# The mixer layers' token-major groups claim their PSUM banks one by one, with ScalarE's copies and VectorE's maxima and sums in TensorE's bank order

## What is computed

```python
m_t = jnp.maximum(inter, dmat.max(axis=-1))
sw = jnp.exp(dmat - m_t[..., None]) * jnp.einsum('bhntk,bhnsk->bhnts', qc, kc)
num = einsum(sw, vc) + s_inter[..., None] * einsum(qc, c_prev)
h = num / jnp.maximum(jnp.abs(den), jnp.exp(-m_t))[..., None]
```

## Time and profile before

| | |
|---|---|
| median of 3 runs | 3080.92 us (3078.48 to 3084.71) |
| span of the profiled execution | 3079.1 us |
| TensorE busy | 97% of the span, 14046 matmuls |
| VectorE, ScalarE, GpSimd busy | 48%, 21%, 65% |
| DMA | mean 89 GB/s |

### The profile page before, as it was taken

One profiled execution on the slowest core, in us unless ns is written; L12 is line 12 of the kernel. 1 busy time (PEld: TensorE's weight loads), 2 busy tenths in 40 slices (PEclk: granted clock), 3 DMA queues, 4 the chain that ended last, 5 costly groups with the idle time before them and its releaser, 6 DMA issues.

```text
span 3079.1 us, 37943 instructions
## 1 busy us (share of the span) xinstructions
PE 2987.8 (97%) x14046; PEld 2451.0 (80%) x14046; DVE 1466.0 (48%) x2397; ACT 649.8 (21%) x1436; POOL 1999.0 (65%) x2041
## 2 busy tenths in 40 slices
PE   8989999999999998999999999999999999999998
PEld 6867778788888877778788888778878888888886
DVE  6668784533324777876443322566321221224543
ACT  3256333200001336433210000000111121211000
POOL 6755454877777766444777777787766555555775
PEclk9999999999999999999999999999999999999999
DMA  4322221433333322222333333233333223222332
GB/s 148 97 69 65 66 68 56 133 92 95 96 94 127 96 83 79 63 63 61 114 96 95 95 95 103 89 96 101 92 95 99 74 82 96 76 83 69 96 96 75
DMA packets 87066, 274.65 MB, mean 89 GB/s; under 512 B 10384, under 2 KB 11024, under 8 KB 86928
## 3 DMA queue, kind: packets, MB, share of 16 engines
q1 hardware_dynamic: 85392, 270.71, 28.7%
q10 hardware_dynamic: 1536, 2.10, 0.3%
HBM read 266.48 MB, written 4.19 MB: 88 GB/s over the span
## 4 chain that ended last, share of the span: by engine, by line
PE 89%; DVE 7%; ACT 2%; issue 1%; POOL 0%; DMA 0%; DVEq 0%; SPq 0%; ACTq 0%; POOLq 0%
PE PS L495 59%; PE PS L544 13%; PE PS L774 5%; PE PS L782 3%; PE PS L845 2%; PE PS L822 1%; PE PS L833 1%; PE PS L1069 1%; PE PS L508 1%; ACT TB L1179 1%; PE PS L1044 0%; DVE SMALLS L1694 0%; PE PS L1036 0%; DVE SQ L1726 0%; PE PS L582 0%
## 5 line engine op out<-in xcount | busy, mean ns | idle before, releaser
L465 POOL TENSOR_TENSOR WL<-RAW,WH 128x512 fp32r<-128x512 f32 (+2 forms) x538 | 796.9, 1481 | 9.8
L457 POOL TENSOR_TENSOR POOL_C<-POOL_C 128x1 f32<-128x1 f32 x538 | 128.5, 239 | 1011.5 <-PE PS L495 580.2
L495 PE MATMUL PS<-XNH,WH 128*128 128x512 f32 x1752 | 693.5, 396 | 3.1 <-DVE OQK L2257 1.6
L495 PE MATMUL PS<-XNL,WH 128*128 128x512 f32 x1752 | 684.3, 391 | 0.0
L462 POOL TENSOR_TENSOR WL<-RAW,WH 128x512 fp32r<-128x512 f32 x420 | 582.8, 1388 | 35.0
L458 POOL TENSOR_SCALAR WH<-RAW 128x1024 fp32r<-128x1024 f32 (+3 forms) x538 | 529.6, 984 | 0.6 <-issue 0.3
L495 PE MATMUL PS<-XNH,WL 128*128 128x512 f32 x1752 | 434.3, 390 | 0.1
L495 PEld LDWEIGHTS PS<-XNH,WH 128*128 128x128 f32 x1752 | 328.9, 188 | 76.1 <-issue 8.2
L495 PEld LDWEIGHTS PS<-XNL,WH 128*128 128x128 f32 x1752 | 329.2, 188 | 71.1 <-issue 3.1
L495 PEld LDWEIGHTS PS<-XNH,WL 128*128 128x128 f32 x1752 | 327.5, 187 | 69.6 <-POOL WL L465 1.0
L544 PE MATMUL PS<-WH,XNH 128*128 128x512 f32 x704 | 279.8, 398 | 7.0 <-ACT VEXT L1179 2.9
(11 more groups left out here) (375 smaller groups left out, 4548.1 us busy)
## 6 DMA issues: line engine op xcount, KB each, us to landing
RAW<-w_oslot SPq DMA_DIRECT2D x56, 512.0 KB, 3.6
RAW<-w_L0ffn SPq DMA_DIRECT2D x44, 512.0 KB, 3.6
RAW<-w_L1ffn SPq DMA_DIRECT2D x44, 512.0 KB, 3.6
RAW<-w_od SPq DMA_DIRECT2D x32, 512.0 KB, 3.6
RAW<-w_L0G SPq DMA_DIRECT2D x24, 512.0 KB, 3.6
RAW<-w_L1G SPq DMA_DIRECT2D x24, 512.0 KB, 3.6
RAW<-w_epg SPq DMA_DIRECT2D x16, 512.0 KB, 3.6
RAW<-w_eug SPq DMA_DIRECT2D x16, 512.0 KB, 3.6
```

Source lines behind the costliest of these rows:

```text
L457: nc.gpsimd.tensor_tensor(POOL_C[:, 1:2], POOL_C[:, 0:1], POOL_C[:, 0:1], ALU.add)
L465: nc.gpsimd.tensor_tensor(WL[:, half, at_:w], RAW[:, slot, at_:w], WH[:, half, at_:w].bitcast(F32), ALU.subtract).then_inc(S("weights_spli ...
L495: mm = nc.tensor.matmul(bank, w[:, slot, k * cols:(k + 1) * cols], x[:, k0 + k, :], start=first and j == 0 and w is WH and x is hi, stop=l ...
```

## The change

`token_group` no longer claims its four banks ahead; each tile claims its own before its first high pass. `spread_u(0)` is issued within the `mo` group, before its last chunk. The second `kvup` group uses the banks in the order 1, 4, 2, 3 and `dv` in the order 5, 0, 1, 4, and ScalarE's copies follow. In the loop `n1` goes to bank `b`, out of which the turned weights were just copied, in place of bank 1. ScalarE copies the turned weights of tile 0 ahead of the key scalings, and the first two `dk` tiles ahead of the exponentials of tile 2. VectorE does `maxima(0)` before the last tile of `dq`, `total` before `maxima` and `state`, and reads `n2` before it rotates a tile of `sk`.

```diff
@@ by_tokens, token_group (TensorE)
-            def by_tokens(outs, c, slot, ks, cols, hi, lo, n_k, shared=False, tiles=range(NT)):
+            def by_tokens(outs, c, slot, ks, cols, hi, lo, n_k, shared=False, tiles=range(NT), banks=None):
                 for w, n in turns:
+                    if banks is not None and w is WH:
+                        claim(banks[n])
             def token_group(name, banks, cols=T, k_per=2, n_k=KD, hi=XNH, lo=XNL, at=0, halfway=None):
-                claim(*banks)
                 for q in range(n_k // k_per):
                     by_tokens([PS[b][:, 0:cols] for b in banks], c, c % 2,
-                              range(q * k_per, (q + 1) * k_per), cols, hi, lo, n_k)
+                              range(q * k_per, (q + 1) * k_per), cols, hi, lo, n_k,
+                              banks=banks if q == 0 else None)
@@ layer (TensorE)
-                token_group(f"L{li}mo", (1, 2, 3, 4))
...
-                spread_u(0)
+                token_group(f"L{li}mo", (1, 2, 3, 4), halfway=lambda: spread_u(0))
...
-                token_group(f"L{li}kvup", (1, 2, 3, 4), k_per=2, n_k=2, hi=CKVH, lo=CKVL, at=1)
+                token_group(f"L{li}kvup", (1, 4, 2, 3), k_per=2, n_k=2, hi=CKVH, lo=CKVL, at=1)
...
-                    claim(1, 0)
+                    claim(b, 0)
                     pe.wait_ge(*L("swt_copied", n + 1))
                     for h in range(M_HEADS):
-                        mm = nc.tensor.matmul(PS[(1, 0)[h // 2]][:, h % 2 * 129:h % 2 * 129 + 129],
+                        mm = nc.tensor.matmul(PS[(b, 0)[h // 2]][:, h % 2 * 129:h % 2 * 129 + 129],
-                    release[1] = release[0] = L("tot_ready", n + 1)
+                    release[b] = release[0] = L("tot_ready", n + 1)
...
-                token_group(f"L{li}dv", (0, 1, 4, 5))
+                token_group(f"L{li}dv", (5, 0, 1, 4))
@@ layer (ScalarE); the copies out of kvup and dv follow the new bank orders too
                 for n in range(NT):
-                    if n:
-                        step_exponentials(n)
                     if n == 2:
                         chunk(seg("dkA") + 4)
                         for m in range(2):
                             run(DKR[:, m, :], PS[4 + m][:, :], ACT.Copy, L("dk_raw"), scale=RTOK[:, m:m + 1])
+                    if n:
+                        step_exponentials(n)
...
                     if n == 0:
                         root("sk", squares=False)
-                        act.wait_ge(*L("rk_ready", 1))
-                        scale_keys(0)
                     act.wait_ge(*L("swt_ready", n + 1))
                     if n:
                         act.wait_ge(*L("n1_ready", n))
                     run(SWT, PS[6 + n % 2][:, :], ACT.Copy, L("swt_copied"))
+                    if n == 0:
+                        act.wait_ge(*L("rk_ready", 1))
+                        scale_keys(0)
@@ layer (VectorE)
-                squares(S_HEADS, "dq")
-                dq_tables = rope_tables(row("dq_g"), 1)
-                for n in range(NT):
-                    norm_tile(DQR, n, RSH, dq_tables, "dq")
...
-                    for e, b in enumerate((1, 0)):
+                    for e, b in enumerate((6 + n % 2, 0)):
...
-                maxima(0)
+                squares(S_HEADS, "dq")
+                dq_tables = rope_tables(row("dq_g"), 1)
+                for n in range(NT):
+                    if n == NT - 1:
+                        maxima(0)
+                    norm_tile(DQR, n, RSH, dq_tables, "dq")
...
                 for n in range(NT):
                     if n:
+                        total(n - 1)
                         maxima(n)
-                        total(n - 1)
                         state(n - 1)
...
-                    if n < NT - 1:
-                        dve.wait_ge(*L("k_scaled", 8 * n + 8))
-                        norm_tile(TA, n, None, sk_tables, "sk")
                     if n:
...
                         dve.wait_ge(*L("n2_taken", n))
+                    if n < NT - 1:
+                        dve.wait_ge(*L("k_scaled", 8 * n + 8))
+                        norm_tile(TA, n, None, sk_tables, "sk")
```

More of the change, by code:

```diff
@@ L640, in layer @@
                             lambda f: L("ckv_low", f + 1))
-                token_group(f"L{li}mo", (1, 2, 3, 4))
-                for n, b in enumerate((1, 2, 3, 4)):
-                    release[b] = L("mo_ready", n + 1)
                 def spread_u(n):
@@ L650, in spread_u @@
                     release[6 + n % 2] = L("ub_taken", n + 1)
-                spread_u(0)
+                token_group(f"L{li}mo", (1, 2, 3, 4), halfway=lambda: spread_u(0))
+                for n, b in enumerate((1, 2, 3, 4)):
+                    release[b] = L("mo_ready", n + 1)
                 pe.wait_ge(*L("iq_turned", 1))
@@ L665, in layer @@
                     release[b] = L("sk_raw", n + 1)
-                token_group(f"L{li}kvup", (1, 2, 3, 4), k_per=2, n_k=2, hi=CKVH, lo=CKVL, at=1)
-                for n, b in enumerate((1, 2, 3, 4)):
+                token_group(f"L{li}kvup", (1, 4, 2, 3), k_per=2, n_k=2, hi=CKVH, lo=CKVL, at=1)
+                for n, b in enumerate((1, 4, 2, 3)):
                     release[b] = L("sv_ready", n + 1)
@@ L745, in layer @@
                             lambda f: L("tr_copied", f + 10))
-                token_group(f"L{li}dv", (0, 1, 4, 5))
-                for n, b in enumerate((0, 1, 4, 5)):
+                token_group(f"L{li}dv", (5, 0, 1, 4))
+                for n, b in enumerate((5, 0, 1, 4)):
                     release[b] = L("dv_ready", n + 1)
```

## The result

The changed kernel takes 3062.0 us (median of 4, 3060.7 to 3064.6) beside 3079.8 us of the kernel before (4 runs on the same chip, 3078.5 to 3084.7): ratio 0.9942, interval 0.9928 to 0.9956. It is 17.8 us faster. The forecast was 33.8 us, and 3062.0 lies 2 us beyond the end of its range.

The account below looks back on a forecast made before the run. It took TensorE, busy 2987.8 of 3079.1 us, as the bound. Gains of 16.0 (`mo` and `kvup`), 15.2 (loop) and 2.6 (first gate) made 33.8 us off, 3045.3, stated as a 3047 us median, range 3039 to 3060.

Parts of the forecast that it names:

- Start of mo and kvup: Groups ahead of the mLSTM loop: TensorE's waits go and `kvup` runs at full clock, 16.0 us gained.
- The loop: mLSTM loop over four token tiles: new order ends it at 46.6 us, gaining 9.1 and 6.1, together 15.2 us.
- By it the maxima, reading PSUM, keep their length in the new place: `maxima(0)` moved before the last `dq` tile: by the skill's two-SBUF-input rule, PSUM-reading maxima are not held off by GpSimd.
- Putting `total` ahead of `maxima` costs the maxima nothing: VectorE's loop order: the spread that the maxima read is issued after the product that `total` waits for; no cost.
- The walk's sum: Tile-by-tile timing of the mLSTM loop in the new order, from the end of `kvup`: 46.6 us.
- rival 1: VectorE bounds the loop and GpSimd's splits stretch it: loop 49.5 us in both layers, 3054 us; chance 0.16.
- Against: Objection to rival 1: in the loop before, most rotations' instructions were at their short length; no size given.
- The first gate: First gate after the loop: bank 5, now copied first of `dv`, removes most of its wait; gain 2.6 us.
- The clock: Without an idle stretch ahead, the `kvup` pair should run at full clock: 2.37 and 1.76 us gained.
- under 0.97: Sign that the forecast is wrong: a granted TensorE clock below 0.97 in the loop.
- rival 2: TensorE's clock falls again because new short waits in the loop come close together: 3060 us; chance 0.09.
- rival 3: Slower: a lasting clock fall in the loop; at 60% slow the time is 3101 us; chance 0.03.

Follow-up runs that it names:

- e6_total_late: The changed kernel with VectorE doing `maxima` ahead of `total` again: 3083.9 us, ratio 1.0014.
- e7_norm_early: The changed kernel with the key (`sk`) rotation ahead of the reading of `n2` again on VectorE: 3062.1 us, ratio 0.9938.
- e4_nolow: The changed kernel with only 8 columns of the `dk` weights' low parts computed on GpSimd, so its result is incomplete: 3051.1 us, ratio 0.9905.
- e5_before_nolow: The kernel before with only 8 columns of the `dk` weights' low parts computed on GpSimd: 3079.7 us, ratio 0.9995.
- e1_front: The kernel before with only the changes ahead of the loop (claims, `spread_u(0)`, `kvup` bank order, early `maxima(0)`): 3066.0 us, ratio 0.9952.
- e3_gate: The changed kernel with GpSimd's splits of three key chunks held until that tile's maxima are done: 3063.1 us, ratio 0.9940.
- e8_gate_hall: The changed kernel with three GpSimd splits held, `HALL` scaling moved to ScalarE, and `dk` sums ahead of the `HALL` products with `MO`: 3057.8 us, ratio 0.9923.
- e11_dv_order: The changed kernel with the `dv` banks in the old order 0, 1, 4, 5: 3065.6 us, ratio 0.9950.
- e2_loop: The kernel before with only the loop's changes and the new `dv` order, everything ahead of the loop as before: 3084.4 us, ratio 1.0011.

## Why the prediction was wrong, step by step

**Start of mo and kvup: right.** 14.9 us of 16.0 in the trace, and 14.8 us as a version of its own (there with loops 3.3 us shorter and a gate 2.1 us longer in it). `mo` lost its wait whole. `kvup` kept 0.41 us for ScalarE's copy out of its first bank, which the sum had at nothing. The maxima of tile 0 took 4.15 us in the new place, against 3.12, beside work of GpSimd: harmless there, but the same thing as in the loop.

**The loop: the step that failed.** The sum took the maxima at 3.03 us and masked product to masked product at 11.7 us, on the ground that "By it the maxima, reading PSUM, keep their length in the new place". Only the two instructions that read the bank do. Ten of the thirteen are 128x4 products and maxima out of SBUF, most with two SBUF inputs, and they took up to 1.28 us for 0.15. The rule on two SBUF inputs (the Trainium skill, SBUF — State Buffer, "Who interferes with whom") speaks of exactly these; the trace agrees with it, and the prediction had left these ten out. Measured: 4.6, 6.2 and 6.8 us for tiles 1 to 3 in layer 0 (3.12 by this measure in tile 3 before), and 14.9 and 15.2 us from one L707 to the next (209.15, 224.03, 239.19 for their starts). The trace of before already spoke against it: the forecast took tile 3's length for all, and tile 1 of layer 0 had taken 4.9 us. What brought the maxima onto the splits is that they start 1 us later against GpSimd, and the gap was 3.6 us wide. In tile 3 `total` makes 0.67 us of that, so the sentence "Putting `total` ahead of `maxima` costs the maxima nothing" is wrong there; but e6_total_late (stretched without it) and e7_norm_early (short with it) point to the key rotation behind the reading of `n2`. The forecast counted the rotation's own time and not what the maxima behind it would meet. e4_nolow and e5_before_nolow show the size: 11 us of the missing 16. The walk's sum was good to half a microsecond (46.1 for 46.6) once that was removed, in part by luck, since its tile 1, 1.0 us too late, made up for rounds that were 0.6 us too short.

This was rival 1, in a harder form: 54.5 and 50.8 us for its 49.5. Its "Against" (most rotations ran at their short length) looked at rotations, and where they had stood: not at the maxima, and not at where the change puts them.

**The first gate: mis-sized.** Forecast 2.6, measured 0.8. The `dv` order helps (1.9 us more waiting when undone), but the copies had been taken as tied to TensorE. They are tied to VectorE: it ends the `dk` sums, ScalarE's 7.76 us of scalings follow, and the copies come last. A shorter loop ends TensorE's work earlier; where that chain doesn't come forward as much, part of the gain turns into this wait: 1.46 to 2.5 us in e1_front, 4.5 in e3_gate, where the held splits fell onto the chain. In e4_nolow, with most of those splits gone, the chain came forward with the loop and the wait stayed at 0.8.

**The clock.** 1.00 in `kvup` and 0.97 and 0.93 in the loop, "under 0.97" being one of the wrong signs. Both loops of e3_gate and of e4_nolow stayed at 1.00, with waits of up to 2.0 and 1.4 us; every loop with a wait of 2.7 us or more fell, to 0.87 and 0.86 with three of about 5 us in each (e6_total_late). In between the runs don't draw a border: layer 0 of e8_gate_hall ran at 0.97 with nothing longer than 2.02, as did layer 1 of the kernel before with 2.07, and layer 1 of e5_before_nolow with 1.91. So rival 2 came in part, through the long waits of rival 1 and not through the shortest ones, which e4_nolow passed at full clock. The lasting low clock of rival 3 was not seen.

**Left open.** How much of the layer 0 to layer 1 spread (54.49 and 50.78, maxima of tile 3 at 6.81 and 3.13) is chance of where GpSimd stands was not settled: e11_dv_order has 5.5 in tile 3 in both layers, e7_norm_early 3.1 in both. In layer 1 of the kernel after, the key rotation was done at 1181.31, before the spread of tile 3 (1181.38), so that the maxima began 1.06 us after it and ended before the split; why it was ahead there stays open. Nor was it traced why e1_front and e2_loop fall short of the whole by 6.6 us when added; e2_loop's own runs spread as widely as that.

## What to carry to other kernels

Moving an instruction in time moves it against every engine, not only along its own queue: for each moved group, lay the other engines' timeline at the new place beside it and reprice, above all small SBUF-only VectorE instructions beside GpSimd's streaming ones. When a wait of TensorE is removed, follow the engine that it waited for to its next deadline; the gain may come back there (6.8 of 7.0 us in e3_gate, none in e4_nolow). Cutting the suspected work in both the old and the new kernel (e4 and e5) is a cheap way to tell an interaction from plain cost. And a length taken from one tile of a loop should be looked up in all of them.

## What the runs showed of the hardware that was not expected

A VectorE instruction of four numbers a partition with two SBUF inputs took 0.15 us alone and 0.88 to 1.28 where it met one of GpSimd's instructions of 1.04 to 1.29 us. In the tiles shown it ended within 0.03 us of that instruction's end, so what it lost was what GpSimd had left of its own, whatever the size of the VectorE instruction. The one behind it often ran at 0.15 again (232.24 and after). In one group of thirteen this came to 3.7 us. A product of 256 elements in the same company took 1.3 to 1.5 us (0.42 alone), hardly more than the 128x4, so many small instructions lose far more in proportion than a few large ones. TensorE's clock held at 1.00 through both loops of e3_gate, with waits of 0.9, 1.6 and 2.0 us in three tiles each; with the same waits it fell to 0.97 in layer 0 of e8_gate_hall.
